# Filling the expert rows in another stage, and computing the decay and beta products in column groups

## What is computed

```
proj = u @ w_in                      # 1024 -> 2304 (q,k,v) + 768 (z) + 6 (a) + 6 (b) + 256 (qm)
qkv  = silu(conv4(qkv)); q, k = l2_normalize(q), l2_normalize(k)
g    = -exp(a_log) * softplus(a + dt_bias);  beta = sigmoid(b)
o    = gated_delta_rule(q, k, v, g, beta, state)      # chunks, one state per head
```

## Time and profile before

| what | us |
|---|---|
| median of three runs | 1746.2 |
| span of the profiled execution | 1739.1 |
| TensorE busy in it | 1475.6 (85%) |
| VectorE / ScalarE / GpSimd busy | 617.6 / 384.5 / 226.5 |
| stage of the in-projection, first to last matmul | 55.8 to 238.1 |
| first matmul of the stage after it | 253.97 |
| prompt's delta rule | 317.4 to 475.6 |

### The profile page before, as it was taken

One profiled execution on the slowest core, in us unless ns is written; L12 is line 12 of the kernel. 1 busy time (PEld: TensorE's weight loads), 2 busy tenths in 40 slices (PEclk: granted clock), 3 DMA queues, 4 the chain that ended last, 5 costly groups with the idle time before them and its releaser, 6 DMA issues. The chain is left out here.

```text
span 1739.1 us, 23072 instructions
## 1 busy us (share of the span) xinstructions
PE 1475.6 (85%) x9105; PEld 1003.8 (58%) x9105; DVE 617.6 (36%) x1410; ACT 384.5 (22%) x996; POOL 226.5 (13%) x227
## 2 busy tenths in 40 slices
PE   6999869899988886998886799999977977998880
PEld 3788756799966445554442566666655454554440
DVE  3455412456356114132111643445523141231114
ACT  2244203344422110111011212223413010111111
POOL 0000011111141001222221100001100001222213
PEclk9999969899976997999897899999988987999995
DMA  9611270000054527899995510403432466999984
GB/s 315 181 73 73 72 154 0 1 1 2 9 194 147 218 78 274 329 384 384 396 400 205 190 62 5 177 1 122 182 142 102 168 239 229 378 393 401 397 314 175
DMA packets 106935, 328.99 MB, mean 189 GB/s; under 512 B 19189, under 2 KB 59997, under 8 KB 81951
## 3 DMA queue, kind: packets, MB, share of 16 engines
q1 hardware_dynamic: 90546, 275.43, 43.1%
q0 software_dynamic: 15040, 47.74, 7.7%
q10 hardware_dynamic: 1248, 4.46, 0.6%
HBM read 301.46 MB, written 41.84 MB: 197 GB/s over the span
## 5 line engine op out<-in xcount | busy, mean ns | idle before, releaser
L1948 PE MATMUL pp<-ring,uT 128*64 128x256 f32 x1728 | 231.0, 410 | 35.6 <-issue 25.3
L1948 PEld LDWEIGHTS pp<-ring,uT 128*64 128x64 f32 x1728 | 124.4, 141 | 132.7 <-issue 65.9
L559 PE MATMUL pp<-uT,ring 128*128 128x272 f32 x576 | 135.2, 393 | 0.9 <-PEq L359 0.9
L559 PEld LDWEIGHTS pp<-uT,ring 128*128 128x128 f32 x576 | 108.0, 190 | 22.2 <-issue 1.0
L1630 PE MATMUL pp<-ring,uT 128*128 128x512 f32 x256 | 113.5, 606 | 4.2 <-PEq L135 4.2
L1969 PE MATMUL pp<-ring,uT 128*64 128x512 f32 x432 | 103.2, 598 | 1.2 <-ACT uT L1999 1.2
L1993 ACT ACTIVATE uT<-pp 128x128 f32<-128x128 f32 x64 | 17.7, 277 | 380.0 <-PE pp L1948 380.0
L1987 DVE COPY uT<-pp 128x128 f32<-128x128 f32 x64 | 18.6, 291 | 233.0 <-PE pp L1958 233.0
L2124 POOL DMA_INDIRECT expert_rows<-uT,row_of_slot x64 | 64.7, 1011 | 246.0 <-ACT uT L1999 242.2
L1630 PEld LDWEIGHTS pp<-ring,uT 128*128 128x128 f32 x256 | 49.7, 195 | 66.8 <-issue 66.8
L1936 PE MATMUL pp<-consts 64*128 64x64 f32 x512 | 70.3, 281 | 18.3 <-DMA consts<-normed_rows,token_of_slot 18.3
(11 more groups left out here) (603 smaller groups left out, 2483.7 us busy)
## 6 DMA issues: line engine op xcount, KB each, us to landing
ring<-in_w_exp_gate SPq DMA_DIRECT2D x54, 1024.0 KB, 21.3
ring<-in_w_exp_up SPq DMA_DIRECT2D x54, 1024.0 KB, 27.7
ring<-in_w_exp_down SPq DMA_DIRECT2D x54, 1024.0 KB, 27.7
ring<-in_w_in_a SPq DMA_DIRECT2D x4, 3072.0 KB, 11.4
scaled_rows<-in_w_exp_gate SPq DMA_DIRECT2D x10, 1024.0 KB, 25.4
scaled_rows<-in_w_exp_up SPq DMA_DIRECT2D x10, 1024.0 KB, 29.6
expert_rows<-zero_rows SPq DMA_DIRECT2D x4, 2048.0 KB
scaled_rows<-in_w_exp_down SPq DMA_DIRECT2D x10, 512.0 KB, 22.2
```

The source lines that it names most:

```text
L559: TE.matmul(pp[n % 2][:, at], w[:, j, ct * P:(ct + 1) * P], uT[:, j, t], start=(j == 0), stop=(j == DJ - 1))
L1948: ins = TE.matmul(pp[0][q * SLOTS:(q + 1) * SLOTS, b * 512:b * 512 + 2 * P], xT[b][:, j, :], w[:, :, j, q, :], start=(j == 0), stop=(j == ...
```

## The change

- The zero tile, its memset on GpSimd and SP's eight zero-writing DMAs leave the in-projection stage. SP gets a list in the prompt's delta rule instead: one DMA writes all 49 x 64 rows of `ys` from the first 1024 columns of the constants (finite numbers), and SP waits for it there.
- The 268 "rest" columns of weights get a tile of their own, `w_rest`, loaded at the stage's start; ring slot 0 is not used for them.
- The products for `a` and `b` are computed with the weights stationary: 32 columns of `w_rest` (the 12 and 20 that are not used) as weight and 128 tokens streamed, the four token chunks in the four column groups of 32, so that the result has channels on the partitions; two transposes bring it back. They come right after the 18th tile's product and the turning of the 17th, before the last `turn`. The order after them is: first query group, the last turn, second query group, the two transposes.
- ScalarE's scratch tile for squares is now part of the new tile `ab_T`.

The diff, cut to its core:

```
-                sp.wait_ge(s_zrow, 1)
-                for q in range(4):
-                    sp.dma_start(ys[NE * SLOTS:, q * 256:(q + 1) * 256].rearrange("(j s) d -> s j d", s=SLOTS), bc(zero[:], 1, OVER)).then_inc(s_st, 16)
-                for n, (slot, name, a, b) in enumerate((((0, "v", 1536, Z0)), (1, "z", Z0, R0), (0, "rest", R0, R0 + NR))):
+                sp.dma_start(w_rest[:], w_in[:, :, R0:R0 + NR]).then_inc(s_wr, 16)
+                for n, (slot, name, a, b) in enumerate((((0, "v", 1536, Z0)), (1, "z", Z0, R0))):
...
-                for q in range(4):
-                    sp.dma_start(ys[0:NE * SLOTS, q * 256:(q + 1) * 256].rearrange("(j s) d -> s j d", s=SLOTS), bc(zero[:], 1, NE)).then_inc(s_st, 16)
...
-                sp.wait_ge(s_st, 160)
+                sp.wait_ge(s_st, 32)
...
-                turn(NT - 1)
-                arrived(pe, "rest")
-                w = slot3(0, NR)
-                pe.wait_ge(s_raw, NT)
-                for pr in range(2):
+                def queries(pr):
+                    if pr == 0:
+                        pe.wait_ge(s_raw, NT)
+                    else:
+                        pe.wait_ge(s_abk, 1)
...
-                pe.wait_ge(s_tok, NT)
-                for c, r in enumerate(ROWS):
-                    for j in range(DJ):
-                        ins = TE.matmul(pp[2][:r, c * 12:(c + 1) * 12], uT[:, j, offset(c):offset(c) + r], w[:, j, 0:12], ...)
+                pe.wait_ge(s_wr, 16)
+                pe.wait_ge(s_raw, NT - 1)
+                for j in range(DJ):
+                    for c in range(NC_P):
+                        TE.matmul(pp[0][32 * c:32 * c + 32, 0:P], w_rest[:, j, 0:32], uT[:, j, offset(c):offset(c) + P], ...)
+                for j in range(DJ):
+                    ins = TE.matmul(pp[0][0:32, P:P + NS], w_rest[:, j, 0:32], uT[:, j, SEQ:T], ...)
+                ins.then_inc(s_ab, 1)
+                queries(0)
+                turn(NT - 1)
+                queries(1)
+                pe.wait_ge(s_tok, NT - 1)
+                TE.transpose(pp[2][:, 0:P], abT[:, 0:P], ident)
+                TE.transpose(pp[2][0:NS, P:P + NS], abT[0:32, P:P + NS], ident[0:32, 0:32]).then_inc(s_abt, 1)
...
+            @block.sync          # in the prompt's delta rule
+            def _(sp):
+                sp.dma_start(ys.rearrange("(j s) d -> s j d", s=SLOTS), bc(consts[0:SLOTS, 0:D], 1, NE + OVER)).then_inc(s_ys, 16)
+                sp.wait_ge(s_ys, 16)
```

More of the change, by code:

```diff
@@ L507, in build @@
         cache_in, cache_out = cache[0:24, :], cache[32:59, :]
-        zero = sb("zero_rows", [SLOTS, D // 4], where=IN)
-        squares = sb("squares", [P, P], where=IN)
+        w_rest = sb("rest_weights", [P, DJ, NR], where=IN)
+        abT = sb("ab_T", [P, P + NS], where=IN)
+        squares = abT[:, 0:P]
         w_out = I["w_out_a"][0].rearrange("(j p) n -> p j n", p=P)
@@ L512, in build @@
         with nc.Block() as block:
-            s_c, s_mm, s_raw, s_ch, s_sum, s_silu, s_tail, s_tr, s_tok, s_free, s_z, s_st, s_zero, s_zrow, s_sq = (
-                sem(f"in_{m}") for m in ("cache", "product", "raw", "chain", "summed", "silu", "tail", "turned", "rows", "slot_free", "rest", "stored", "zeroed", "zero_row", "squares"))
+            s_c, s_mm, s_raw, s_ch, s_sum, s_silu, s_tail, s_tr, s_tok, s_free, s_z, s_st, s_zero, s_sq = (
+                sem(f"in_{m}") for m in ("cache", "product", "raw", "chain", "summed", "silu", "tail", "turned", "rows", "slot_free", "rest", "stored", "zeroed", "squares"))
+            s_wr, s_ab, s_abk, s_abt = (sem(f"in_{m}") for m in ("rest_weights", "ab_product", "ab_kept", "ab_turned"))
             @block.sync
@@ L530, in _ @@
                 sp.dma_start(O["cache_conv_sample"][0].rearrange("b r c -> (b r) c"), cache_out[3:27, :]).then_inc(s_st, 16)
-                sp.wait_ge(s_st, 160)
-            @block.gpsimd
-            def _(pool):
-                G.memset(zero[:], 0.0).then_inc(s_zrow, 1)
+                sp.wait_ge(s_st, 32)
             @block.tensor
@@ L564, in _ @@
                         turn(n - 1)
-                    if ct == 5:
+                    if ct == 5 and g < 2:
                         pe.wait_ge(s_mm, n + 1)
                         pe.sem_inc(s_free, 1)
-                turn(NT - 1)
-                arrived(pe, "rest")
-                w = slot3(0, NR)
-                pe.wait_ge(s_raw, NT)
-                for pr in range(2):
+                def queries(pr):
[3 more added lines that the diff above has]
+                        pe.wait_ge(s_abk, 1)
                     for t, at in HALVES:
                         for j in range(DJ):
-                            ins = TE.matmul(pp[1 - pr][:, at], w[:, j, 12 + pr * P:12 + (pr + 1) * P], uT[:, j, t], start=(j == 0), stop=(j == DJ - 1))
+                            ins = TE.matmul(pp[1 - pr][:, at], w_rest[:, j, 12 + pr * P:12 + (pr + 1) * P], uT[:, j, t], start=(j == 0), stop=(j == DJ - 1))
                     ins.then_inc(s_z, 1)
-                pe.wait_ge(s_tok, NT)
-                for c, r in enumerate(ROWS):
-                    for j in range(DJ):
-                        ins = TE.matmul(pp[2][:r, c * 12:(c + 1) * 12], uT[:, j, offset(c):offset(c) + r], w[:, j, 0:12], start=(j == 0), stop=(j == DJ - 1))
-                ins.then_inc(s_z, 1)
+                pe.wait_ge(s_wr, 16)
+                pe.wait_ge(s_raw, NT - 1)
+                for j in range(DJ):
+                    for c in range(NC_P):
+                        TE.matmul(pp[0][32 * c:32 * c + 32, 0:P], w_rest[:, j, 0:32], uT[:, j, offset(c):offset(c) + P], start=(j == 0), stop=(j == DJ - 1))
+                for j in range(DJ):
+                    ins = TE.matmul(pp[0][0:32, P:P + NS], w_rest[:, j, 0:32], uT[:, j, SEQ:T], start=(j == 0), stop=(j == DJ - 1))
+                ins.then_inc(s_ab, 1)
[5 more added lines that the diff above has]
+                TE.transpose(pp[2][0:NS, P:P + NS], abT[0:32, P:P + NS], ident[0:32, 0:32]).then_inc(s_abt, 1)
             @block.vector
@@ L614, in _ @@
                     V.tensor_copy(crow[:, k, 3:27].rearrange("p (b r) -> p b r", b=DB), sv[:, :, 4:7]).then_inc(s_tail, 1)
+                dve.wait_ge(s_ab, 1)
+                chain(V.tensor_copy(abT[:, 0:P], pp[0][:, 0:P]))
+                V.tensor_copy(abT[0:32, P:P + NS], pp[0][0:32, P:P + NS]).then_inc(s_abk, 1)
                 for pr in range(2):
@@ L618, in _ @@
                     chain(V.tensor_copy(all_tokens(qmT[:, pr, :]), halves(pp[1 - pr])))
-                dve.wait_ge(s_z, 3)
+                dve.wait_ge(s_abt, 1)
                 dve.wait_ge(s_zero, 5)
-                chain(V.tensor_copy(ab[:, 0:NC_P, :], pp[2][:, 0:12 * NC_P].rearrange("p (c k) -> p c k", c=NC_P)))
-                chain(V.tensor_copy(ab[0:NS, NC_P, :], pp[2][0:NS, 12 * NC_P:12 * NCH]))
+                chain(V.tensor_copy(ab[:, 0:NC_P, :], pp[2][:, 0:P].rearrange("p (c k) -> p c k", c=NC_P)[:, :, 0:12]))
+                chain(V.tensor_copy(ab[0:NS, NC_P, :], pp[2][0:NS, P:P + 12]))
             @block.scalar
@@ L640, in rows @@
                                 act.wait_ge(s_sq, i)
-                            S.activation(squares[:], tok[g][:, c, ct * P:(ct + 1) * P], ACT.Square, accum_out=ss[:, g, c, ct:ct + 1]).then_inc(s_sq, 1)
+                            S.activation(squares, tok[g][:, c, ct * P:(ct + 1) * P], ACT.Square, accum_out=ss[:, g, c, ct:ct + 1]).then_inc(s_sq, 1)
                 for n in range(NT):
@@ L1011, in build @@
         s_zero = sem("state_zero")
+        s_ys = sem("expert_rows_filled")
         def group(t, g, rows=P):
```

## The result

The changed kernel takes 1715.26 us (median of four runs, 1712.68 to 1718.07) against 1746.43 us before: 0.9829 of the time, 95% interval 0.9809 to 0.9848. The gain of the medians is 31.2 us, where 30.3 was predicted. The profiled execution has a span of 1716.3 us, 22.8 less than before; why the two traces lie closer together than the medians is said at the end of the part on why the prediction was right.

The account below looks back on a forecast made before the run. The prediction took the in-projection's end to be bound by a DMA wait, stores queued behind the fills, and a TensorE tail ahead of it. Gains of 27.8 + 2.5 = 30.3 us gave 1716 us, range 1712 to 1720 (chance 0.78).

Parts of the forecast that it names:

- The wait at the barrier: End of the in-projection: TensorE's 15.85 us wait for SP's stores shrinks to 0.5 us after the last copy.
- Rival 2: In-projection's end: the cache stores are slow themselves, 14.2 us of the gain are lost, 1730 us; chance 0.05.
- The products: In-projection's tail: the new products for a and b take 3.8 us, bounds 2.6 to 9.2.
- rival 1: In-projection's tail is longer: column groups do not overlap or the clock falls, 1725 us; chance 0.08.
- Queries and last turn: In-projection's tail: two query groups with the last turn between them, 7.50 + 0.71 + 7.50 = 15.7 us.
- First term: In-projection's end: shorter TensorE tail and barrier wait start the next stage at 226.2 instead of 253.97, gain 27.8 us.
- The clock at the next stage's start: First z parts after the in-projection: they run at full clock, 10.53 instead of 13.04 us, gain 2.5 us.
- The fill in the delta rule: Prompt's delta rule: the 12.85 MB fill takes 67 us, hidden in 158.2 us, and costs 0.
- Rival 3: Delta rule: the fill slows its small matmuls and copies, 10% over 67 us, 6.7 us, 1723 us; chance 0.05.
- The upper bound of 1.3%: Delta rule: most that contention with the fill could cost, 0.9 us over 67 us, 2.1 over the stage.
- Rival 4: Delta rule: the one big fill outlasts it, SP holds the barrier 110 us more, 1826 us; chance 0.03.
- the first two terms of the sum: The 27.8 us at the in-projection's end and the 2.5 us at the next stage's start.

Follow-up runs that it names:

- three fills: The changed kernel with the same fill made three times, one after the other, in the delta rule: 1746.19 us in one run.
- the tail alone: The changed kernel with the fills put back where the kernel before had them, at the in-projection's start and after the 18th tile's product: 1741.57 us, 0.9966.
- the shift by 32: The changed kernel with the whole first query group computed twice, 32 more product records: 1720.40 us, 0.9866 of the kernel before.
- the shifts above: The changed kernel with half or all of the first query group computed twice, 16 or 32 more product records: 1711.79 and 1720.40 us.

## Why the prediction was right

Point by point, from the two traces:

- *The wait at the barrier.* Predicted 0.5 us from the last copy to the next stage; measured 226.28 - 225.73 = 0.55. The cache stores were issued at 218.2 (predicted 218.0); the last landed 4.1 us after its issue, ahead of VectorE's last copy. Rival 2 (the stores are slow themselves) is out: 0.27 us instead of 10.95.
- *The products.* Predicted 3.8 us, measured 208.87 - 206.50 = 2.4, just under the lower bound of 2.6, for which the prediction shows no working. The row of line 205 was taken as it stood; its length goes with the columns (1.87 us for 128 of 192, measured 1.95). The sample's part took 0.6 where 1.0 was put. The clock stayed at 1.00 under these products and under the queries behind them, so rival 1 is out. Each of the 64 records took 30 ns. "TensorE: Matmul & The Clock Gate", section "Wait — 56ns, not 53.3ns?", in the Trainium skill gives two floors for short matmuls, about 25 ns in any case and about 62 ns with hardware decode off. The 30 ns keep to the first; a matmul of the code, two records, took 61 ns, and no run here shows which of the two the second would count.
- *Queries and last turn.* Predicted 15.7 us, measured 224.30 - 208.87 = 15.4. First term in all: predicted 27.8, measured 49.31 - 19.98 = 29.3.
- *The clock at the next stage's start.* Predicted 2.5 us, measured 13.04 - 10.40 = 2.6. The reason given was half of it: besides the idle time, the 12-column products lowered the clock, so that both had to go. That was seen only in the runs with one of the two: 13.4 and 13.2 us with the products, 265.22 - 251.90 = 13.3 with the idle time.
- *The fill in the delta rule.* Predicted 67 us (measured 64.4) and no cost: from the stage's first matmul to the next stage's store pass 476.01 - 317.41 = 158.6 us before and 443.88 - 285.37 = 158.5 after, and its work takes 158.3 under three fills. The section "SBUF: two separate sides" of "SBUF — State Buffer" in the Trainium skill, by which DMA and engine accesses don't contend, agrees with that. Rival 3 is out. The upper bound of 1.3% was read from rows that don't show contention: 7.60 us stand also at 208.87 in the changed kernel, where the DMA share is 0.00, and in the kernel before a group took 7.50 in the middle of the fills (a timeline row and a window of it):

```profile
71.83 7.50 PE L559 MATMUL pp<-uT,ring 128*128 128x272 f32 x32
```

```profile
74.00:78.00 4.00, 4.00 (x19) 3.32 (x18) 1.96 (x5) 2.12 (x8) 0.00 (x0) 1.00 0.88 194
```

- *Rival 4.* One DMA over 64 partitions stayed at 200 GB/s, as the fills had. The section "Door 1: The DMA port swizzle" of the same page says that partitions 0 to 63 reach 8 of 16 ports; 64.4 against 33.0 us agrees. So the prediction misread the limit: the engines' busy share of 0.88 did not mean that they could move no more, since from 128 partitions they moved 399 GB/s. Its price for the fill, taken from the measured 192 GB/s, was right all the same.

The two parts need each other: the fill alone brings 14.3 us (1745.86 - 1731.55), the tail alone 4.3 (1745.86 - 1741.57), both with the clock 28.7 to 31.2 (the changed kernel beside them and in the result).

*The profiled executions differ by 22.8 us only.* Up to the delta rule's start the changed kernel is 317.41 - 285.37 = 32.0 us ahead, and it is still so at its end. In this, 1.6 us were lost before the 18 tiles' end: its first product ran at a clock of 0.50 from 56 to 58 us, where the kernel before had 1.00. And 1.7 us came from a z part at the stage's end: it took 5.41 us in all four traces whose z parts began at 0.50, and 3.72 here and in six of the other seven, so that it may be a second part of the clock term; no run separates the two. Then the sample stage takes 80.9 instead of 75.0 us, and the rest 3.4 us more. The loss at the start and that in the sample stage are clock levels that don't follow the change: the shift by 32, the same program up to its queries, ran its first product at 1.00 and the run with only the fill moved at 0.50, and the sample stage is the one of the shifts above. What decides the level there stays open.

The medians differ by more because of which executions were profiled. A time on record stands about 2 us above its span, so the 1739.1 us before belong to a run of some 1741, 5 us under its median, and the changed kernel's is the run of 1718.07, 2.8 over its median; its four runs fall into two pairs, 1712.7 and 1718.0. The two together are nearly all of the 8.4 us between 22.8 and 31.2. So the first two terms of the sum are confirmed to 1.5 us, while the agreement of 30.3 with 31.2 in the whole is good to about 3 us and in part luck.

## What to carry to other kernels

Before shortening what an engine does at the end of a stage, look at what holds the barrier: with 8.4 MB of fills queued ahead of two small stores, 15 us less on TensorE were worth 4, and the fills moved away were worth 14. Put a bulk write where its landing is waited for by no one, and judge the place by its length against the work beside it (64 in 158 us), not by how empty the queues are. Turning a product round so that the narrow side is the weight, in column groups, paid twice here: the products themselves were 8 us shorter, and the stage behind them no longer began at the low clock.

## What the runs showed of the hardware that was not expected

- A DMA from 64 partitions moved 200 GB/s with rows of 4 KB as with rows of 1 KB (192); from 128 partitions it took 33.0 us for 12.6 MB, about 380 GB/s. The DMA engines showed a busy share of 0.88 to 0.98 at the half rate and 1.00 at the full one, so that share doesn't tell a limit on the other side.
- Products with 12 columns streamed lower the granted clock to 0.50 although TensorE is never idle and the DMA engines are (234 to 238 us in the run with only the fill moved), and the stage behind them starts at it.
- The same stage of 434 records took 72.1 to 80.9 us over the twelve traces, with its mean granted clock between 0.69 and 0.79; a program with 3.75 us more work in front of it was not slower.
